# A transformer block's opening re-staged: square sums on token rows, column-tiled modulation products, and one weight slab moved behind the attention

## What is computed

```python
ml = split(silu(c)     @ ada_w[i] + ada_b[i], 6)     # 6 vectors of 1024 for the latents
mc = split(silu(c_ctx) @ ada_w[i] + ada_b[i], 6)     # and for the context
h  = x * rsqrt(mean(x * x, -1) + 1e-6) * norm_g * (1 + m[1]) + m[0]
y  = attention(h) @ w_o
x  = x + m[2] * y                                    # m[2] is the gate
```

## Time and profile before

| | |
|---|---|
| time, median of 3 runs | 2893.48 us (2887.86 to 2895.68) |
| time of the profiled execution | 2893.03 us |
| its span in the profile | 2891.1 us |
| PE busy | 2714.8 us (94%) |
| DVE, ACT, POOL busy | 1032.9, 663.4, 533.0 us |
| PE's busy share in 40 slices of 72.3 us | `6699999797999999998999999999787999999997` |
| opening and first normalisation | 0 to 100.4 us |
| projection behind the attention | 569.8 to 654 us |

### The profile page before, as it was taken

How to read it: one execution, slowest core, us unless ns; L and a number is a source line. 1 busy time by engine, 2 the same in 40 slices (tenths; PEclk the granted TensorE clock), 3 DMA queues, 4 the chain that set the end, 5 groups by cost and what they waited for, 6 DMA issues and landing times. The chain is left out here.

```text
span 2891.1 us, 46368 instructions
## 1 busy us (share of the span) xinstructions
PE 2714.8 (94%) x18878; PEld 1832.5 (63%) x18879; DVE 1032.9 (36%) x2322; ACT 663.4 (23%) x1391; POOL 533.0 (18%) x472
## 2 busy tenths in 40 slices
PE   6699999797999999998999999999787999999997
PEld 6355555454555555554777667776646878687784
DVE  5244544416677664113444444444311110010100
ACT  0243444302222220014322333232112110010000
POOL 0111111013333224221323222232110100000000
PEclk6899999898999999998999999999787999999999
DMA  6142242203333343101011100110009996594831
GB/s 222 45 122 68 64 111 59 91 0 94 110 112 106 116 122 80 50 13 36 15 31 31 31 23 9 31 31 9 31 29 357 341 319 190 179 302 146 264 100 30
DMA packets 309235, 297.74 MB, mean 103 GB/s; under 512 B 5712, under 2 KB 268880, under 8 KB 308944
## 3 DMA queue, kind: packets, MB, share of 16 engines
q1 hardware_dynamic: 303024, 273.30, 30.9%
q0 software_dynamic: 4896, 17.83, 2.4%
q10 hardware_dynamic: 1152, 4.19, 0.4%
HBM read 281.14 MB, written 12.58 MB: 102 GB/s over the span
## 5 line engine op out<-in xcount | busy, mean ns | idle before, releaser
L1702 PE MATMUL bank<-work,weight_ring 128*128 128x128 f32 (+1 forms) x2048 | 314.7, 316 | 6.1 <-ACT work L1752 6.1
L2115 PE MATMUL bank<-hidden,weight_ring 128*128 128x512 f32 (+1 forms) x768 | 309.6, 537 | 1.8 <-ACT work L2437 1.8
L1702 PEld LDWEIGHTS bank<-work,weight_ring 128*128 128x128 f32 x2048 | 291.2, 193 | 27.6 <-issue 8.1
L685 PE MATMUL bank<-weight_ring,hidden 128*128 128x384 f32 x760 | 266.6, 495 | 4.8 <-ACT work L814 4.6
L1250 PE MATMUL bank<-hidden,weight_ring 128*128 128x384 f32 x704 | 238.7, 493 | 11.1 <-PEq L1238 11.1
L1391 DVE SCALAR_TENSOR_TENSOR weight_ring<-weight_ring,silu_c 128x256 f32<-128x256 f32 x308 | 218.9, 751 | 5.5
L685 PEld LDWEIGHTS bank<-weight_ring,hidden 128*128 128x128 f32 x760 | 138.0, 191 | 108.9 <-ACT work L814 16.6
L1250 PEld LDWEIGHTS bank<-hidden,weight_ring 128*128 128x128 f32 x704 | 133.2, 192 | 99.8 <-PEq L1238 11.4
L2115 PEld LDWEIGHTS bank<-hidden,weight_ring 128*128 128x128 f32 x768 | 135.4, 190 | 82.7 <-issue 68.6
L1250 PE MATMUL bank<-weight_ring 128*128 128x384 f32 x528 | 181.7, 495 | 0.5 <-DVE work L1399 0.5
L1857 DVE TENSOR_TENSOR work<-work,bank 128x128 f32<-128x128 f32 (+1 forms) x88 | 29.8, 338 | 425.2 <-ACT work L1757 425.2
(11 more groups left out here) (344 smaller groups left out, 3783.9 us busy)
## 6 DMA issues: line engine op xcount, KB each, us to landing
weight_ring<-in_moe_w_in SPq DMA_DIRECT2D x64, 1024.0 KB, 10.1
weight_ring<-in_ada_w SPq DMA_DIRECT2D x38, 1024.0 KB, 5.2
weight_ring<-in_ffn_w_in SPq DMA_DIRECT2D x44, 512.0 KB, 4.9
hidden<-in_moe_w_out SPq DMA_DIRECT2D x8, 2816.0 KB, 10.5
residual<-in_moe_w_out SPq DMA_DIRECT2D x8, 2816.0 KB, 16.0
work<-in_moe_w_in SPq DMA_DIRECT2D x16, 1024.0 KB, 8.8
weight_ring<-in_na_w_qkv SPq DMA_DIRECT2D x24, 512.0 KB, 7.5
weight_ring<-in_gdn_w_qkv SPq DMA_DIRECT2D x24, 512.0 KB, 5.4
```

Of the source, the lines that this page charges most:

```text
L685: mm = nc.tensor.matmul(m.psum[6][:, 0:3 * P], m.H[:, k, t * P:(t + 1) * P], weights(u)[:, k, :], start=(k == 0), stop=(k == KD - 1))
L1702: mm = nc.tensor.matmul(B[c % 4][:, ab * HALF:ab * HALF + N], w[:, ab, k, (c % 2) * P:(c % 2 + 1) * P], XG[:, k, 0:N], start=(k == 0), sto ...
L2115: mm = nc.tensor.matmul(B[b][:, c0:c0 + t1 - t0], W[:, s, k, :], m.H[:, k, t0:t1], start=(k == 0), stop=(k == KD - 1))
```

## The change

1. The table of constants is laid out anew: identity, epsilons, the 2-column picker and token numbers come first (138 columns, loaded at the start), the rest (2089 columns) is loaded behind the slabs. The 128-column mean matrix shrinks to one column, a block that nothing used goes.
2. `load_and_modulation` and `norm_modulate` become one Block, `load_and_norm`. As each token tile lands, ACT squares its rows with an accumulated sum (128 x 1024 to one column) besides PE's transposes, which now use four banks. One root and one inverse on 128 x 6; PE spreads them out by six matmuls; DVE writes the scaled residual into `m.H`.
3. The four slabs of layer 0 (order 2, 3, 0, 1) go to two places in `work` and to slots 2 and 3, and are multiplied on PE in column tiles as in the attention, ACT copying and PE summing each. Then ACT and DVE each apply scale and shift to half of the tiles.
4. `m.sc32` gets memory of its own and is built in the opening; its build and wait in the attention go.
5. SP issues the slabs, the late constants, the attention's weights and bias in this one Block.
6. The early slab of layer 1 leaves the opening. It is loaded to slot 2 at the start of the projection and multiplied there on PE in column tiles, behind the fourth group. The group order becomes 0 1 2 3 5 6 7 4, to keep banks 0 and 1 free for it.

```diff
-        load_and_modulation(m)
-        norm_modulate(m, "n0", 0, 0, ahead=attention_ahead(m))
+        load_and_norm(m, ahead=attention_ahead(m))
         neighbourhood_attention(m, ahead=projection_ahead(m, "no", dram["na_w_o"]))
-        project_to_residual(m, "no", 0, 0)
+        project_to_residual(m, "no", 0, 0, load=early_slab(m), early=True)
```

The opening's new lists, cut to their core:

```diff
+        def _(sp):
+            sp.dma_start(m.small[:, :], dram["small"]).then_inc(small_in, 16)
+            sp.dma_start(m.const[:, 0:C_EARLY], dram["const"][:, 0:C_EARLY]).then_inc(small_in, 16)
             for t in range(6):
                 sp.dma_start(raw[:, t, :], src).then_inc(tile_in[t], 16)
+            for j, s in enumerate(SLABS):
+                sp.dma_start(slabs[j], adaw[:, :, s * BANK:(s + 1) * BANK]).then_inc(slab_in[j], 16)
+            sp.dma_start(m.const[:, C_EARLY:C_ALL], dram["const"][:, C_EARLY:C_ALL]).then_inc(const_in, 16)
+            ahead(sp)
+            sp.wait_ge(const_in, 16)
...
+        def _(pe):
+            pe.wait_ge(inverted, 1)
+            for bank, (t0, t1, _) in zip((B_LAT, B_CTX), parts):
+                for t in range(t0 // P, t1 // P):
+                    mm = nc.tensor.matmul(B[bank][:, t * P - t0:(t + 1) * P - t0], ss[:, t:t + 1].to_broadcast([P, P]), ident, start=True, stop=True)
+                mm.then_inc(spread, 1)
+            for j, s in enumerate(SLABS):
+                pe.wait_ge(slab_in[j], 16)
+                for kk in range(2):
+                    for q in range(4):
+                        mm = nc.tensor.matmul(B[j][32 * q:32 * q + 32, :], m.sc32[:, 2 * q + kk, :], slabs[j][:, 2 * q + kk, :], start=(kk == 0),
+                                              stop=(kk == 1), skip_group_check=True)
+                mm.then_inc(ada_product, 1)
+                pe.wait_ge(ada_copied, j + 1)
+                for g in range(4):
+                    mm = nc.tensor.matmul(B[B_STAT][:, at:at + 2], ada_rows[:, g * P:(g + 1) * P], const(m, C_FOUR, 2), start=True, stop=True)
+                mm.then_inc(ada_summed, 1)
...
+        def _(act):
+            for t in range(6):
+                act.wait_ge(tile_in[t], 16)
+                nc.scalar.activation(junk, raw[:, t, :], ACT.Square, accum_out=ss[:, t:t + 1]).then_inc(squared, 1)
+                act.wait_ge(turned, 2 * t + 2)
+                nc.scalar.copy(m.X[:, 4:8, t * P:(t + 1) * P], B[(2 * t + 1) % 4][:, :].rearrange("p (k t) -> p k t", k=4)).then_inc(odd_out, 1)
+                act.wait_ge(squared, t + 1)
+            nc.scalar.activation(ss, ss, ACT.Sqrt, bias=const(m, C_EPS, 1), scale=1.0 / D).then_inc(root, 1)
+            for j in range(4):
+                act.wait_ge(ada_product, j + 1)
+                nc.scalar.copy(ada_rows, B[j][:, :]).then_inc(ada_copied, 1)
+            act.wait_ge(mod_scale, 1)
+            for t0, t1, v in reversed(parts):
+                for k in range(0, KD, 2):
+                    nc.scalar.activation(m.H[:, k, t0:t1], m.H[:, k, t0:t1], ACT.Identity, ...)
```

And in the projection:

```diff
+                if early and e == 3:
+                    pe.wait_ge(m.early_in, 16)
+                    pe.wait_ge(added, added_0 + len(parts))
+                    for kk in range(2):
+                        for q in range(4):
+                            mm = nc.tensor.matmul(m.psum[0][32 * q:32 * q + 32, :], m.sc32[:, 2 * q + kk, :], ada_slab[:, 2 * q + kk, :],
+                                                  start=(kk == 0), stop=(kk == 1), skip_group_check=True)
+                    mm.then_inc(ada_product, 1)
+                if early and e == 4:
+                    pe.wait_ge(ada_copied, 1)
+                    for n in range(4):
+                        mm = nc.tensor.matmul(m.psum[1][:, 2 * n:2 * n + 2], ada_rows[:, n * P:(n + 1) * P], const(m, C_FOUR, 2), start=True, stop=True)
+                    mm.then_inc(ada_product, 1)
```

More of the change, by code:

```diff
@@ new lines, in _ @@
+            for t in range(6):
+                dve.wait_ge(turned, 2 * t + 1)
+                nc.vector.tensor_copy(m.X[:, 0:4, t * P:(t + 1) * P], B[(2 * t) % 4][:, :].rearrange("p (k t) -> p k t", k=4)).then_inc(even_out, 1)
+            dve.wait_ge(root, 1)
+            nc.vector.reciprocal(ss, ss).then_inc(inverted, 1)
+            dve.wait_ge(even_out, 6)
+            dve.wait_ge(odd_out, 6)
+            for k in range(KD):
+                for b, (t0, t1, _) in enumerate(parts):
+                    dve.wait_ge(spread, b + 1)
+                    nc.vector.tensor_tensor(m.H[:, k, t0:t1], m.X[:, k, t0:t1], B[(B_LAT, B_CTX)[b]][:, 0:t1 - t0], ALU.mult).then_inc(scaled, 1)
@@ L403, in square_sums @@
+            for t0, t1, v in reversed(parts):
+                for k in range(1, KD, 2):
+                    nc.vector.tensor_scalar(m.H[:, k, t0:t1], m.H[:, k, t0:t1], m.MODA[:, 0, 0, k, v:v + 1], m.MOD[:, 0, 0, k, v:v + 1], ALU.mult,
+                                            ALU.add).then_inc(hidden, 1)
 def square_sums(m):
@@ L1011, in _ @@
         def _(act):
-            for g in range(KD):
-                act.wait_ge(added, (g + 1) * len(parts))
-                if g > 1:
-                    act.wait_ge(collected, collected_0 + g - 1)
-                nc.scalar.activation((m.sq if g else m.sq_sum)[:, first:TOK], m.X[:, g, first:TOK], ACT.Square).then_inc(squared, 1)
+            for e, g in enumerate(ORDER):
+                act.wait_ge(added, added_0 + (e + 1) * len(parts))
+                if e > 1:
+                    act.wait_ge(collected, collected_0 + e - 1)
+                nc.scalar.activation((m.sq if e else m.sq_sum)[:, first:TOK], m.X[:, g, first:TOK], ACT.Square).then_inc(squared, 1)
+                if early and e == 3:
+                    act.wait_ge(ada_product, 1)
+                    nc.scalar.copy(ada_rows, m.psum[0][:, :]).then_inc(ada_copied, 1)
         @block.gpsimd
         def _(pool):
-            for g in range(1, KD - 1):
-                collect_squares(m, pool, sums, g, first)
+            for e in range(1, KD - 1):
+                collect_squares(m, pool, sums, e, first)
         if load:
@@ L1029, in _ @@
         def _(pe):
-            for g in range(KD):
-                pe.wait_ge(w_in[g // 4], 16)
-                if g >= 4:
-                    pe.wait_ge(added, (g - 3) * len(parts))
+            for e, g in enumerate(ORDER):
+                pe.wait_ge(w_in[g // 4], w_in_0 + 16)
+                if e >= 4:
+                    pe.wait_ge(added, added_0 + (e - 2 if early else e - 3) * len(parts))
+                if early and e == 7:
+                    pe.wait_ge(ada_copied, 1)
+                    pe.wait_ge(mod_sum, 1)
                 ws = slot(m, g // 4).rearrange("p (k n) -> p k n", k=KD)
```

242 lines of the change are left out of this document (86 added, 156 removed).

## The result

The changed kernel takes 2849.3 us in the median of four executions (2844.2 to 2849.6), the kernel before 2893.2 (2887.9 to 2895.7): ratio 0.9847 with a 95% interval of 0.9829 to 0.9864, about 44 us or 1.5% faster. The prediction was 2845 in 2837 to 2856. The profiled execution of after is the fastest of its four: 2844.2 us, span 2842.4, so its trace shows 48.7 us less span than the trace of before.

The account below looks back on a forecast made before the run. The prediction took the opening's serial work before the attention's first matmul, at 100.44 us, as the bound: 51.0 us gained there, 2.8 lost in the projection, -48.2 in all, from 2893.03 to 2845 us, range 2837 to 2856.

Parts of the forecast that it names:

- The opening: Up to the attention's first matmul: moves from 100.4 to 49.4 us, 51.0 us gained.
- Landings: Opening's loads: smaller front load of constants moves everything behind it 3.1 us earlier; fourth slab lands at 37.8 us.
- Rival (b): Opening: landings don't move, tiles keep their own pace, or late constants slow the slabs; 3.1 us later, 2848; chance 0.10.
- Clock: PE's clock during the slabs' products: last sums ready at 43, a mixture between 41.5 (full) and 48.0 (half throughout).
- rival (a): Opening: half clock throughout the slabs, PE the bound to 48.0; 4.7 us later, 2849.5; chance 0.25.
- Covered normalisation: Opening: root and inverse by 19.9, scalings by 31 us, hidden under the slabs; without cover about 13 us.
- Scale and shift: End of the opening: ACT keeps eight of sixteen calls, 4.85 us instead of 9.69, DVE doing eight beside it.
- SP's last issue: End of the opening: SP's held-back queue issues the attention's bias by 49.0 us, almost together with ACT's end.
- some 2760 pieces under way: SP's queue in the opening: limit on 2 KB pieces; weight loads all issued 6.0 us after 40.6.
- The early slab: Projection: products 1.9 and sums 0.9 count in full, 2.8 us lost; load, copy and bias add hidden.
- rival (d): Tiling mode switches on PE cost 0.42 us twice per slab, last and early slab: 1.7 us more, 2846.5; chance 0.04.
- Rival (e): Projection: the early slab lands so late that PE's wait eats the gain; slower than before, above 2893; chance 0.02.

Follow-up runs that it names:

- early_only: Kernel before with only the early slab moved from the opening to the projection; median 2893.2 us, ratio 1.0004 to before.
- const_whole: Changed kernel with the whole table of constants loaded at the start again, none behind the slabs; median 2849.4 us, first matmul at 52.8.
- spread_last: Changed kernel with PE's spread of the inverse root moved behind the products of all four slabs; median 2854.7 us, first matmul at 57.7.
- a_again: The changed kernel run again with no edit; median 2848.6 us, ratio 0.9852 to before, first matmul at 51.9.
- columns_only: Kernel before with early slab moved and four slabs multiplied in column tiles, normalisation left a Block of its own; median 2874.8 us, first matmul at 76.1.
- best: Changed kernel with longer filler matmuls, second pair's attention weights issued later, scale and shift split six ACT, ten DVE; median 2844.0 us, ratio 0.9826 to before.
- warm: Changed kernel with filler matmuls into an unused bank to keep PE working in the opening; median 2850.3 us, first matmul at 50.0.
- warm_sp: Changed kernel with the fillers of warm, and the second pair's attention weights issued at the attention's start; median 2849.1 us, first matmul at 50.0.

## Why the prediction was right, point by point

**The opening, 51.0 us forecast, 49.0 measured.** Right in its mechanism: the serial pieces that went had been on the path. The exception is DVE's third slab, whose work ended at 57.6 beside PE's own products at 57.2 in before, so that only its sums counted (3.9 us in early_only). Two terms were mis-sized.

- Landings. Forecast 3.1 us for the constants, measured 1 to 1.4 for nine tenths of them (const_whole), because "the queue is full from there to the slabs" at 386 GB/s is wrong: the windows show 232 to 279 GB/s from 2 to 5 us and about 258 under the tiles. Against before the last tile came 2.0 us sooner and the first slab 2.2 (22.08 in spread_last against 24.30). The spacing of the slabs was missed too: in spread_last, whose loads are those of after, three of them take 17.4 us (22.08 to 39.49), not 16.6. Both together are the 1.7 us by which the fourth slab, forecast at 37.8, was late at 39.5 (39.8 in a_again). Rival (b), given 0.10, was the nearer one by size, and the tiles' own pace of 240 GB/s that it names is about what the windows show; still the tiles do move, by less. Its other half, late constants that slow the slabs, isn't borne out: columns_only loads nothing behind its slabs before 45.12 and has 17.6 us between the same two (23.15 to 40.72).
- Clock. I took 43 for the last sums, a mixture. They were ready at 45.5, and 1.7 of these 2.5 us are the landing: the clock itself cost little more than the mixture had allowed. The last slab ran at half clock from a backlog of 0.9 us. It wasn't rival (a), an unbroken chain at half clock to 48.0: the second slab's products ran at full level and the third waited 2.2 us for its slab. From 39.6 and at full clock it would be 43.3, as "best" has it from its landing (38.92 to 42.6). One of the rows behind this term was misread: from the end of the transposes at 20.16 to the fall at 23.9 are 3.8 us, not 3.9.
- Covered normalisation: root and inverse by 20.7 (forecast 19.9), scalings by 30.6 (forecast 31). The cover's worth was put at 13 us; the part that spread_last uncovered, spread and scalings, measures 8.6; squares and root stayed covered there.
- Scale and shift 4.85 forecast, 4.89 measured. SP's last issue forecast at 49.0, measured at 49.8. That looks nearer than it is: the late constants landed at 42.4, not 40.6, and 6.0 us behind that the last weight issue would have ended at 48.4, where it ended at 47.4. So the estimate of some 2760 pieces under way, or the rate taken with it, is 1 us off. And SP wasn't last, ACT was; it became last in warm.

**The early slab, 2.8 us forecast, 2.95 measured** (89.11 - 86.16), 2.4 by its removal. No new wait appeared. From the products' start to the next group's are 1.85 us, against 1.71 of streaming at 2.4 GHz, so rival (d), which asked for 0.84 more, is out. The Trainium skill's rule of draining between tiling modes ("TensorEngine Tiling (Array Packing)", Key Properties) may hold, but its price is inside those 0.14 us. Rival (e) had nothing behind it: the slab lands 8.1 us after its issue at 521.0, and PE asks for it at 564.2.

**The sum.** -48.2 forecast for the profiled execution, -48.7 in the trace, which is partly luck: the opening gave 2.0 less, the projection took 0.15 more, the attention 0.3 more, and the stages behind were 2.9 shorter, inside their scatter. The medians differ by 43.9, and with a_again by 43.7, about 4.3 less than the forecast. Before's traced execution is a middling one; after's and a_again's are each the fastest of their four. Why the others take up to 9 us more is open, since they have no trace.

## What to carry to other kernels

When several preparations run one behind the other in front of a big stage, find the last landing first and hide the rest under it: here the re-staged normalisation was worth 24 us, of which spread_last shows 8.6 as place alone, and the column tiles for the products 20. Behind a shortened chain the next bounds stand close together (SP's issues at the Block's end, the clock PE has when the last slab lands, the first weights), so a fix for one of them alone gives less than it removes: in warm ACT was done 2.6 us sooner and the first matmul came 1.5 sooner. Read a change of 1% by stages in the trace, and don't compare whole times of kernels whose values reach a router differently.

## What the runs showed of the hardware

- The granted clock fell 1.1 and 0.8 us after PE's last work in after (19.3, 32.9), and 3.8 us after it in before (23.9). With fillers it stayed at full level through a pause of 1.5 us in front of warm_sp's second slab, and fell at 28.3 in a pause of 1.3 us in front of warm's second slab and at 38.8, just behind a pause of 0.75 us, as warm_sp's fourth slab began. The same products then take 1.9 or 3.6 us, from one execution of the same code to the next (third slab: 3.64 in after, 1.92 in a_again).
- A front load of 1.07 MB less brings the following tiles only 0.8 to 1.3 us, at 386 GB/s worth 2.8 (const_whole against after and a_again). The DMA engines are full at about 258 GB/s while the tiles are loaded and at 387 while the slabs are.
- The time that SP spends on issuing depends on what is queued: the same six weight loads of 512 KB took 7.5 us to issue in before, with no slab under way, and 17.6 us in after, behind 8 MB of slabs and the late constants.
